# Mixer output stage: list writes moved behind the retention's inverse roots on POOL, rank products moved behind the scores on TensorE

## The reference, cut to what matters

```python
def retention_chunkwise(q, k, v, log_g, s0, inclusive):   # per chunk of 128 tokens
    scores = jnp.einsum('bnihd,bnjhd->bnhij', qc, kc) * dmat
    intra = jnp.einsum('bnhij,bnjhe->bnihe', scores, vc)
    ...
    cross = jnp.einsum('bnihd,ih,nbhde->bnihe', qc, xi, s_prev)
    return (intra + cross).reshape(B, T, H, dv)

def mixer(...):
    ...
    o = retention_chunkwise(...) + retention_chunkwise(reversed ...)
    y_ret = head_rms(o).reshape(B, T, D_RET) * jax.nn.silu(g)
    out = jnp.concatenate([y_lru, y_ret], axis=-1) @ w_out

def moe(h, w_router, b_router, ...):          # h is the RMS-normed, modulated x + g1 * out
    s = jax.nn.sigmoid(x @ w_router)
    ...                                       # the 4 best of 8 groups, then the 6 best of 64 experts
    gates = sel / jnp.sum(sel, axis=-1, keepdims=True) * ROUTE_SCALE
    routed = routed_experts(x, eidx, gates, w1, w3, w2)
    shared = swiglu(x, ws1, ws3, ws2)
    return routed + shared
```

## Time and profile before

| | |
|---|---|
| median of 3 runs | 2748.6 us (2745.43 to 2749.72) |
| profiled execution | 2750.21 us, of which the span of the trace is 2748.4 us |
| granted TensorE clock, mean | 0.957 of full |
| TensorE matmul busy | 2511.8 us, 91% |
| VectorE, ScalarE, POOL busy | 1740.8, 1009.5 and 983.3 us |
| steps 4 to 15 of `mixer_out` | from about 882 to 1163 us of the span |

### The profile page before, as it was taken

One profiled execution on the slowest core, in us unless ns is written; L12 is line 12 of the kernel. 1 busy time (PEld: TensorE's weight loads), 2 busy tenths in 40 slices (PEclk: granted clock), 3 DMA queues, 4 the chain that ended last, 5 costly groups with the idle time before them and its releaser, 6 DMA issues. The chain is left out here.

```text
span 2748.4 us, 47130 instructions
## 1 busy us (share of the span) xinstructions
PE 2511.8 (91%) x11959; PEld 2031.4 (74%) x11960; DVE 1740.8 (63%) x2738; ACT 1009.5 (37%) x1615; POOL 983.3 (36%) x1008
## 2 busy tenths in 40 slices
PE   7999999998938888849999999999999999999990
PEld 4787777776737777737888888787878878787870
DVE  4663663566325666665647758677785777768683
ACT  3311433343312222221324535355453445545442
POOL 1210025713134656532133433333333333334334
PEclk9999999999969999969999999999999999999995
DMA  7775758675565555336769979889897989979887
GB/s 283 297 274 207 265 208 285 233 263 184 202 221 196 173 173 173 116 110 133 201 182 268 268 190 290 258 255 309 239 305 192 287 267 261 312 191 303 257 245 271
DMA packets 239399, 642.13 MB, mean 234 GB/s; under 512 B 24268, under 2 KB 37904, under 8 KB 223824
## 3 DMA queue, kind: packets, MB, share of 16 engines
q1 hardware_dynamic: 188880, 459.75, 47.0%
q0 software_dynamic: 50432, 181.27, 26.9%
HBM read 463.61 MB, written 177.33 MB: 233 GB/s over the span
## 5 line engine op out<-in xcount | busy, mean ns | idle before, releaser
L2058 POOL DMA_INDIRECT sum_d<-w_shared_raw,give x136 | 234.4, 1723 | 606.2 <-DMA sum_d<-w_shared_raw,give 303.3
L2343 PE MATMUL ps_h<-w_exp_hi,x_exp_t_hi 128*128 (+1 forms) x1216 | 312.1, 399 | 23.1 <-ACT w_exp_hi L2099 21.5
L2343 PE MATMUL ps_h<-w_exp_hi,x_exp_t_lo 128*128 (+1 forms) x1216 | 321.9, 407 | 0.0
L2163 DVE TENSOR_TENSOR w_exp_lo<-w_exp,w_exp_hi (+1 forms) x256 | 307.0, 1219 | 9.3 <-ACT w_exp_hi L2099 4.2
L2343 PE MATMUL ps_h<-w_exp_lo,x_exp_t_hi 128*128 (+1 forms) x1216 | 309.8, 397 | 0.0
L2125 ACT ACTIVATE h_exp_t_hi<-ps_ht 128x256 fp32r<-128x256 f32 x152 | 58.4, 384 | 634.6 <-PE ps_ht L2352 628.5
L2343 PEld LDWEIGHTS ps_h<-w_exp_hi,x_exp_t_hi 128*128 128x128 f32 x1216 | 229.4, 189 | 78.9 <-ACT w_exp_hi L2099 21.7
L1134 PE MATMUL ps_p<-wa_hi,hx_split 128*128 128x512 f32 x1088 | 277.2, 400 | 5.9 <-DVE kvqg_out L100 3.9
L2343 PEld LDWEIGHTS ps_h<-w_exp_lo,x_exp_t_hi 128*128 128x128 f32 x1216 | 229.2, 188 | 55.9
L2099 ACT ACTIVATE w_exp_hi<-w_exp (+1 forms) x256 | 255.4, 1055 | 35.6 <-DMA w_exp<-in_experts 32.3
L2343 PEld LDWEIGHTS ps_h<-w_exp_hi,x_exp_t_lo 128*128 128x128 f32 x1216 | 217.7, 189 | 41.4
(11 more groups left out here) (300 smaller groups left out, 4393.0 us busy)
## 6 DMA issues: line engine op xcount, KB each, us to landing
w_exp<-in_experts SPq DMA_DIRECT2D x386, 512.0 KB
hx_split<-hx_d SPq DMA_DIRECT2D x54, 1024.0 KB, 5.6
rec_m<-rec_d SPq DMA_DIRECT2D x16, 1536.0 KB, 7.2
hx_d<-hx_split SPq DMA_DIRECT2D x18, 1024.0 KB, 6.3
wm_rest<-in_w_mod_rest POOLq DMA_DIRECT2D x16, 1024.0 KB, 5.9
rec_d<-kvqg_out SPq DMA_DIRECT2D x48, 256.0 KB, 4.3
xt<-in_xt POOLq DMA_DIRECT2D x18, 512.0 KB, 8.6
rec_d<-kt_kvf_out SPq DMA_DIRECT2D x32, 256.0 KB, 4.8
```

What stands on the lines that cost most here:

```text
L2058: pool.indirect_dma_start(sum_d[:, :], bass.IndirectOffsetOnAxis(give[:, par:par + 1], 0), y[:, par], None, compute_op=ALU.add).then_inc(a ...
L2163: dve.tensor_tensor(w[1][:, piece(e, i)].bitcast(F32R), raw(e, i), w[0][:, piece(e, i)], ALU.subtract).then_inc(gu_lo, 1)
L2343: last = pe.matmul(out, x[:, j * P:(j + 1) * P].bitcast(F32R), w_part[:, bass.ds(w_at + j * stride, 512)].bitcast(F32R), start=(start and ...
```

## The change

On POOL `enlist` is issued behind the retention's inverse roots `rh` in the same step, and no longer ahead of them. On TensorE `rank` is issued behind y's transposes and the scores, and no longer ahead of them. Nothing else is changed: the same instructions, the same waits, the same data.

```diff
@@ POOL, step(n, par)
                     pool.wait_ge(h2s_done, t + 1)
                     pool.tensor_tensor(h2[:, par], h2[:, par], b2[:], ALU.add).then_inc(h2_done, 1)
-                if on(n, 4):
-                    enlist(pool, R, n - 4, par, list_d)
                 if on(n, 0):
 
                     wait(pool, y_done, n)
@@
                     pool.wait_ge(rh_own, n + 1)
                     pool.tensor_tensor(rh[:], rh[:], mhalf[:].broadcast_to([P, HEADS]), ALU.pow).then_inc(rh_done, 1)
+                if on(n, 4):
+                    enlist(pool, R, n - 4, par, list_d)
@@ TensorE, step(n, par)
                     out_products(0, [t[:, q] for t in yl], 0, True, False)
-                if on(n, 4):
-                    pe.wait_ge(qt_copied, min(n + 1, NT) if isinstance(n, int) else n + 1)
-                    pe.wait_ge(qf_done, min(n + 1, NT) if isinstance(n, int) else n + 1)
-                    wait(pe, carry_done, n - 4)
-                    rank(pe, R, n - 4, ps_q)
                 if on(n, 1):
                     pe.wait_ge(y_done, n)
@@
                         last = pe.matmul(ps_s[:, e], rec[:, par, e], q_t[:, e], start=True, stop=True)
                     last.then_inc(s_done, 1)
+                if on(n, 4):
+                    pe.wait_ge(qt_copied, min(n + 1, NT) if isinstance(n, int) else n + 1)
+                    pe.wait_ge(qf_done, min(n + 1, NT) if isinstance(n, int) else n + 1)
+                    wait(pe, carry_done, n - 4)
+                    rank(pe, R, n - 4, ps_q)
```

## The result

The changed kernel took 2762.47 us (median of 5 runs, 2760.96 to 2765.22), the kernel before 2749.72 us beside it (5 runs, 2745.43 to 2751.66): ratio **1.0051, 95% interval 1.0036 to 1.0066**, 12.8 us slower. 7.2 were forecast.

The account below looks back on a forecast made before the run. Today's 23.43 us loop between inverse roots, with squares held behind list writes, was to give way to POOL's chain at 23.6. Step 4 -3.5, steps +1.9, step 5 +0.7, tail +8.1: +7.2 on 2748.6, 2755.8 us; range 2743 to 2775.

Parts of the forecast that it names:

- POOL's chain: Roots, writes, state, `rstd`, `h2`, sum, roots: the new loop, 23.34 us plus 0.2 for roots meeting `choose`, 23.6 a step.
- the tail: Behind step 15, writes ahead of step 16's `rstd` and a held `yt_done` make it later: +8.1 us, other end +5.0.
- step 5: Starts early and finds POOL late; TensorE waits ahead of h2's transposes, half the half-clock cost falls there: +0.7 us.
- The late squares: ScalarE's squares start 3.58 us behind TensorE's sum; with the writes moved this goes, kept whole once, in step 4: -3.5 us.
- R2: Rival: the hold is not the writes' doing, squares stay 3.58 us late; +43 on the forecast, 2799 us; chance 0.05.
- The second loop: Through VectorE's `choose` and x1 to TensorE's first `yl` products: 22.7 to 23.5 us a step, upper end taken.
- The rank: TensorE's rank behind the scores: about 1.0 us today, but no wait left to remove in the new order: 0.
- The rule of the hold: A TensorE completion signal in the later part of a run of list writes arrives some 1.3 us behind the last write.
- R1: Rival: TensorE's idle time settles ahead of h2's transposes, half clock on the first loop: +15 us, 2771 us; chance 0.13.
- The load of rec: SP's load waits for the state, lands 19.5 us behind the roots; TensorE wants it after 20.7: covered, no cost.
- R3: Rival: writes cost POOL less behind the roots, up to 1.8 us off the first loop: 2740 us; chance 0.14.
- R4: Rival: inside no change, tail at +5.0 or loop at 23.4 us: +2.2 to about +5, 2751 to 2754 us; chance 0.28.

Follow-up runs that it names:

- e8: The changed kernel with six spare 128 x 512 multiplies on GpSimd between h2 and the roots, where the list writes had been: 2797.14 us in one run.
- e4: The changed kernel with the list writes of step 15 alone back ahead of the roots: 2758.26 us, ratio 1.0042 to the kernel before.
- e1: The kernel before with only the list writes moved behind the roots, rank in its old place: 2759.74 us, ratio 1.0063.
- e7: The changed kernel with one spare 128 x 512 multiply on GpSimd behind each step's list writes: 2789.19 us, ratio 1.0147 to the kernel before.
- e5: The changed kernel with the first half of x1 taken ahead of `choose` on VectorE: 2776.46 us, ratio 1.0097 to the kernel before.
- e2: The kernel before with only TensorE's rank moved behind the scores, list writes still ahead of the roots: 2732.71 us, ratio 0.9956.
- e11: e5 with 28 spare transposes on TensorE ahead of h2's transposes in each step from 4 on: 2763.18 us, ratio 1.0074 to the kernel before.
- e3: e2 with three of the six list writes ahead of the roots and three behind, steps 4 to 15: 2726.47 us, ratio 0.9945 to the kernel before.
- e6: e3 with the first half of x1 taken ahead of `choose`: 2717.68 us, ratio 0.9884 to the kernel before.
- e9: e6 with two list writes ahead of the roots and four behind: 2720.66 us, ratio 0.9896 to the kernel before.

## Why the prediction was right, and where it was not

The time lies in the range and on the side forecast, and the mechanism of the steps, POOL's chain as the new loop, held in most of them. The size (+7.2 against +12.8) came out low by one term, the steps (+1.9 against +9.5), and high by two, the tail (+8.1 against +6.1) and step 5 (+0.7 against 0). That it came out on the right side, clear of no change, is in part luck: without the tail, whose reason was wrong, the forecast's terms add up to -0.9 us. Point by point:

- **The late squares go away** (-3.5, once). Right: step 4 went from 22.22 to 18.70 in the profiles compared. Against the three profiles of before it is -3.2. e8 shows that the writes are the cause, so R2 is out. The 3.58 us are not the late signal alone, though: POOL's own queue keeps the roots behind the writes too. In the earlier trace rows the last write ends at 1018.49 and the two instructions of the roots take 1.3 us, so with squares in time they would have ended at about 1019.8 instead of 1022.46 (an estimate from these rows): some 2.7 us are the signal, 0.9 the queue. In e4's step 15, where the square is only 0.71 us late, the roots still wait for the last write.
- **POOL's chain becomes the loop** (23.34 us and 0.2). Right in mechanism for steps 6 to 11: e1 has the whole loss, e7 shows that more work on POOL lengthens the step and e5 that less waiting elsewhere doesn't shorten it. The sum was 0.5 us short. By the step shown: copy and wait for the first write -0.32 (0.99 from the roots' end, 1.31 forecast), writes +0.01, state +0.43 (3.61 for the three instructions, 4.04 measured), `rstd` +0.12, transposes and sum +0.06, square to roots +0.24 (2.64, 2.88 measured), together +0.54 on 23.34 = 23.88, as measured. The term mis-sized is mostly contention. The forecast looked for it at the roots and `choose` only; it is there (0.45 us for the first root instruction beside VectorE's L1274, 0.19 alone), but the larger part is at the state's add beside `yl_lo`, a pair that meets because `qb_t`, `sfd` and `sfs` come 8.4 us later. The Trainium skill, SBUF — State Buffer, Who interferes with whom, covers such a pair, a VectorE instruction with two SBUF inputs and a GpSimd one that reads SBUF; the rows agree (1605 against 1268 ns for the add, 1439 against 685 for `yl_lo`).
- **What the step is compared with** (23.43). The row was right for its profile and high for the kernel: 23.43, 23.04 and 22.90 in three. Against their mean of 23.12, 11 steps cost 11 x (23.98 - 23.12) = +9.5 us and not +2. Of the difference to the forecast's +1.9, 3.4 are this base and 4.2 the 0.38 us by which the step was under-sized (0.28 in POOL's chain, the rest in steps 11 to 15). The steps of before vary because the squares' delay does; the steps behind the change hardly do from profile to profile (23.98, and 23.99 in e1). A distance that rests on such a delay needs more than one profile.
- **Step 5** (+0.7). Wrong in place: 23.64 us, no longer than the others, though TensorE did wait 3.6 us ahead of h2's transposes. They and the sum took 3.77 us, at full clock.
- **The second loop** (x1, 22.7 to 23.5). The gap was forecast at about 3 us and is 2.9, at the `yl` products, with half clock behind it. In steps 6 to 11 it costs nothing, because `h2` comes later than TensorE. In steps 12 to 15 the longer stretch at half clock uses the slack up and TensorE comes 0.4 to 0.8 us too late; that is 0.9 us in all. So the two loops do stand close together, as the forecast had them, but at about 23.9 and 24.1 us, not 23.4.
- **The rank** (0). Right: e1 against after. In the kernel before its old place cost more than the 1.0 us named: e2's steps are 1.5 us shorter than the mean of before.
- **The tail** (+8.1, other end +5.0). The row says +6.1. The reason given was wrong: `yt_done` of step 15 was to be held to 10.0 us behind the roots by the writes. It was not held (transposes' end 1181.78, split 1181.82, the last write under way from 1181.26); the transposes themselves came late, 8.0 us behind the roots instead of some 6, behind the half-clock `yl` products, and e4 shows the writes off this chain. Where x1 comes early (e5, e11) the distance is 9.3 us, close to the 9.5 of the other end.
- **The rule of the hold.** "A completion signal of TensorE that falls into the later part of a run of list writes" arrives late: that is too wide. In the step of after shown above, `ps_yt`'s last transpose ends at 1012.32, when five writes have begun, and ScalarE takes it at 1012.35, 7.0 us behind the roots, where the forecast had 10. In the three profiles of before, 32 of 36 sums are followed by a square 1.1 to 1.4 us behind the last write's end; the other four came earlier, but still 1.3 to 3.6 us late. The moment of the sum's end doesn't decide it either: in step 4 of all three the sum ends 0.9 us behind the start of the third write, and the square comes 3.57, 1.32 and 3.57 us later. Which signals are late, and by what, isn't settled.
- **R1** did not happen, and lies closer than its 0.13 says. After has its idle time at the `yl` products; move 1 us of POOL's work (e7) or x1 (e5) and it settles ahead of h2's transposes, at 1.6 us a step in e5, and at 2.6 in e7 with its 1.1 of work. Its price of up to 1.6 us a step was the right size: e5 loses 1.6.
- **The load of rec.** Covered, as forecast: TensorE's transposes of q never wait for it. The account was wrong. The load doesn't wait for the state of its own step (`sf_done` stands at 1 ahead of the first step, so the count asked for is that of the step before). From step 6 on it is issued 4.4 to 4.8 us behind the roots, behind y, instead of 1.3, and it takes longer to land, 11.0 us in the median against 7.2: it is there 14.2 to 20.0 us behind the roots, and the forecast's 19.5 is near the upper end by luck.
- **R3** is out: behind the roots too the writes start 1.26 to 1.38 us apart. **R4** is out by size.

Balance of the stage: -3.2 (step 4) + 9.5 (steps 5 to 15) + 6.1 (tail) - 0.6 (to the last slots) = +11.8, against +11.7 in the stage; the ratio's interval is 9.9 to 18.1 us.

## What to carry to other kernels

Work moved off a place where it delays a signal lands whole on its engine's chain behind the new place, if the engine has no idle time there: draw the loop with the moved work in it, before counting the delay as gained. When two edits are made together, try each alone: here one cost the time and the other, alone, gained 1.5 us a step (e1, e2). Splitting the work around the place (e3, e6, e9) went with the fastest kernels, but no run here shows what the split adds to e2. An idle gap ahead of work that has slack can keep the half clock off work that has none; before a wait is removed, ask where the idle time goes. A term that stands on a delay from semaphores or DMA wants two or three profiles of the same kernel.

## What the runs showed of the hardware

- Beside a run of six indirect writes of GpSimd (0.96 to 1.08 us each, 1.26 to 1.38 from start to start), ScalarE starts on TensorE's result 1.3 to 4.9 us late; beside 7.5 us of plain GpSimd work 0.03 to 0.04 us (e8). The Trainium skill, SBUF — State Buffer, Who interferes with whom, has PE and ACT never waiting on anyone; for their access to SBUF no run here speaks against it, but ScalarE's start on TensorE's finished result does come late. How, was not found, nor whether it is the signal or ScalarE that is late: the delay is not decided by a write being under way alone (e6: 1.56 and 0.24 us; e4's step 15, with all six writes in the old place: 0.71).
- TensorE idle for 2.3 to 5.4 us was mostly followed by half clock in after, e1, e5 and e7: four `yl` products 2.04 against 1.17 us, h2's eight transposes 1.97 against 1.09. Behind idle time of 0.5 to 0.9 us in after the transposes ran at full clock. Behind 3.59 us in step 5 of after they took 1.09 us as well, so the length of the gap is not all. Ahead of the rank, in the three profiles of before, idle times of 1.8 to 2.5 us were followed by half clock in some steps (the scores then take 1.7 to 1.9 us) and not in others (1.06 us).
- Filling the gap with useless transposes (e11) brought the granted clock from 0.93 and 0.86 up to 1.00 and took 1.9 us off each step.
